# Four-layer fp32 kernel: the convolution's taps all on VectorE, GELU in one piece, and a new order of the steps

## The reference

```python
z = rms_norm_2(x, norm_g) @ w_in
o_a = fox_attention(q, k, v, ff + fox_b) * silu(f_gate)        # 4 heads, causal, with decay
o_b = conformer_conv(glu_in, ...) * silu(c_gate)
o_c = nsa_attention(...) * silu(n_gate)                        # 8 heads, 2 groups, 3 branches
x = x + concat([o_a, o_b, o_c]) @ w_out

def conformer_conv(u, conv_w, conv_b, ln_g, ln_b, w_pw):
    a, b = split(u, 2); y = a * sigmoid(b)                     # 256 channels
    y = causal depthwise convolution of y with 31 taps + conv_b
    return silu(layer_norm(y, ln_g, ln_b)) @ w_pw

def compress(x, pe, w1, w2):      # for k and for v: 15 windows of 32 tokens, in 2 groups
    blk = x[windows] + pe
    return gelu(blk @ w1) @ w2
```

## Time and profile before

| | us |
|---|---|
| median of 3 runs | 1629.15 |
| lowest, highest | 1629.04, 1633.23 |
| the profiled execution | 1630.12 |
| its span, first to last instruction | 1628.2 |
| TensorE busy | 1585.0 |
| VectorE busy | 1066.8 |
| ScalarE busy | 825.1 |
| GpSimd busy | 258.8 |

### The profile page before, as it was taken

How to read it: one execution, slowest core, us unless ns; L and a number is a source line. 1 busy time by engine, 2 the same in 40 slices (tenths; PEclk the granted TensorE clock), 3 DMA queues, 4 the chain that set the end, 5 groups by cost and what they waited for, 6 DMA issues and landing times.

```text
span 1628.2 us, 27282 instructions
## 1 busy us (share of the span) xinstructions
PE 1585.0 (97%) x11240; PEld 1435.0 (88%) x11240; DVE 1066.8 (66%) x1269; ACT 825.1 (51%) x1123; POOL 258.8 (16%) x208
## 2 busy tenths in 40 slices
PE   7999999999999999999999999999999999999997
PEld 7999888888989999999988888898999898879885
DVE  4655557765865555655565867576555589968995
ACT  5443446653454343544454665345444465656563
POOL 0000060010000000000035001000000059405930
PEclk9999999999999999999999999999999999999999
DMA  7757555342555656556746534354656466147512
GB/s 227 231 183 234 177 182 171 124 139 81 179 181 185 203 182 204 168 197 194 237 156 183 163 109 143 106 193 150 218 187 197 124 220 193 33 137 223 192 33 91
DMA packets 206613, 273.97 MB, mean 168 GB/s; under 512 B 18775, under 2 KB 167097, under 8 KB 206009
## 3 DMA queue, kind: packets, MB, share of 16 engines
q1 hardware_dynamic: 206376, 272.67, 52.3%
q10 hardware_dynamic: 144, 0.00, 0.0%
HBM read 271.61 MB, written 1.08 MB: 167 GB/s over the span
## 4 chain that ended last, share of the span: by engine, by line
PE 83%; DVE 11%; ACT 3%; issue 2%; POOL 1%; DMA 0%; SPq 0%; POOLq 0%; ACTq 0%; DVEq 0%
PE bank L506 28%; PE bank L555 14%; PE bank L991 8%; PE bank L980 7%; PE bank L2043 4%; PE bank L1181 3%; DVE wlo L438 3%; PE bank L2299 2%; PE bank L1263 2%; PE bank L2021 2%; PE bank L1124 1%; ACT whi L427 1%; PE bank L1099 1%; DVE hT_lo L357 1%; PE bank L2196 1%
## 5 line engine op out<-in xcount | busy, mean ns | idle before, releaser
L438 DVE TENSOR_TENSOR wlo<-raw,whi 128x2048 fp32r<-128x2048 f32 (+2 forms) x258 | 585.1, 2271 | 327.1 <-ACT whi L427 326.2
L427 ACT ACTIVATE whi<-raw 128x2048 fp32r<-128x2048 f32 (+2 forms) x258 | 484.7, 1881 | 294.2 <-PE bank L555 101.1
L506 PE MATMUL bank<-hT_hi,whi 128*128 128x256 f32 x1408 | 391.6, 278 | 1.3 <-DVE wlo L438 1.0
L506 PE MATMUL bank<-hT_lo,whi 128*128 128x256 f32 x1408 | 389.8, 277 | 0.0
L506 PE MATMUL bank<-hT_hi,wlo 128*128 128x256 f32 x1408 | 389.7, 277 | 0.0
L506 PEld LDWEIGHTS bank<-hT_hi,whi 128*128 128x128 f32 x1408 | 264.7, 188 | 3.0 <-DVE wlo L438 1.8
L506 PEld LDWEIGHTS bank<-hT_lo,whi 128*128 128x128 f32 x1408 | 265.3, 188 | 0.0
L506 PEld LDWEIGHTS bank<-hT_hi,wlo 128*128 128x128 f32 x1408 | 264.7, 188 | 0.0
L555 PE MATMUL bank<-whi,Y 128*128 128x512 f32 (+1 forms) x748 | 224.1, 377 | 0.0
L555 PEld LDWEIGHTS bank<-whi,Y 128*128 128x128 f32 x748 | 140.2, 188 | 28.0
L311 POOL TENSOR_TENSOR st<-st 128x1 f32<-128x1 f32 x18 | 18.0, 1009 | 919.4 <-ACT X L304 919.4
(11 more groups left out here) (398 smaller groups left out, 2824.9 us busy)
## 6 DMA issues: line engine op xcount, KB each, us to landing
raw<-in_ffn_w SPq DMA_DIRECT2D x132, 1024.0 KB, 5.5
raw<-in_w_in SPq DMA_DIRECT2D x80, 1024.0 KB, 5.5
raw<-in_w_out SPq DMA_DIRECT2D x16, 1024.0 KB, 4.9
...
```

The costliest lines, as they stand in the source:

```text
L427: act.activation(m["whi"][:, slot, 0:w], m["raw"][:, slot, 0:w], ACT.Copy).then_inc(s.hi_ready, 1)
L438: dve.tensor_tensor(m["wlo"][:, slot, 0:w], m["raw"][:, slot, 0:w], m["whi"][:, slot, 0:w].bitcast(F32), ALU.subtract).then_inc(s.lo_ready, 1)
L506: mm = pe.matmul(B[bank][:, mt * T:(mt + 1) * T], a, b, start=(n == 0 and k == 0), stop=(n == KK - 1 and k == 2))
```

## The change

Six things change in both second-kind layers.

1. The convolution's half 0 leaves GpSimd. VectorE does all 62 taps. Even and odd taps of each half go to accumulators of their own, four chains in all, and a tap waits only for the tap of its chain; two adds join them. A step `taps.k` now has four operations.
2. GELU for keys and values is one set of operations on 32 x 512 in place of two on 32 x 256.
3. K of the compression is copied, rotated and transposed (`cmp_kt`, a step of its own on TensorE, before `value.0`) ahead of V's copies; the zeros are written much earlier (`cmp_zero`). The ten products of constants go.
4. The scaling and the epsilon of the variance move from GpSimd into VectorE's copy in `ln.1`.
5. VectorE's order: the three maxima of an item stand ahead of taps, `prob.0` comes before `lo.11`, `cmp_score` ahead of `tall.5`, `lo.19` ahead of `ln.1`.
6. ScalarE's order: `exp.0-2` directly behind `hi.10`, both `tok_b` copies and then `gelu` ahead of the turns, `tall.5` behind `turn.2`, and `cmp_prob` behind `exp.5`.

```diff
@@ -110,9 +110,15 @@
         self.eng, self.sem, self.n = eng, sem, 0
 
     def __call__(self, ins):
+        self.until(self.step(ins))
+
+    def step(self, ins):
         self.n += 1
         ins.then_inc(self.sem, 1)
-        self.eng.wait_ge(self.sem, self.n)
+        return self.n
+
+    def until(self, n):
+        self.eng.wait_ge(self.sem, n)
 
 
...
@@ -255,13 +261,13 @@
...
     y_ready=3, ln_var=1, ln_scaled=1, ln_silu=1, ln_split=2, pw_gated=1, pw_split=1, params_in=144,
-    bias_zero=1, conv_step=60, ln_rs=1)
+    bias_zero=1, ln_rs=1)
...
@@ -1855,23 +1861,23 @@
 
 PE2 = words("""
     xt.0 fv.0-1 params fv.2 xt.1 fv.3-15 sm tall.3-4 tall.0 tall.1-2 sg w1.0 scores.0 w1.1 tok.1 tok_b.1 w1.2 tok.0 w1.3
-    tok_b.0 turn.0 tall.5 turn.1 hid_turn turn.2 cmp_kv value.0 heads_turn cmp_score scores.1 tall.6 scores.2 cmp_turn
+    tok_b.0 turn.0 tall.5 turn.1 hid_turn turn.2 cmp_kv heads_turn cmp_kt value.0 cmp_score scores.1 tall.6 scores.2 cmp_turn
     tall.7 turn.3 scores.3 turn.4-5 tall.8 turn.6-7 scores.4 ln.0 turn.8 value.1 ln.1 turn.9 value.2 ln.2 turn.10-11 wo.0-2
     turn.12 wo.3 pw turn.13 wo.8-9 turn.14 wo.10 value.3-4 wo.11 wo.4-6 wo.12-13 wo.7 wo.14-15
 """)
 ACT2 = words("""
-    hh.0-1 sq.1 hh.2-15 hi.2 params hi.3 sm hi.4 decay hi.5 fox_own tall.4 hi.6 tall.0 hi.7 blk.0-1 hi.8 tall.1-2 hi.9-12 exp.0 fv
-    hi.13-14 exp.1 hi.15-16 exp.2 tok_b.1 gelu.0 tok_b.0 turn.0 gelu.1 turn.1 tall.5 hid_turn turn.2 hi.17 heads_turn hi.18
-    cmp_prob exp.3-5 tall.6 cmp_turn exp.6-8 hi.19 tall.7 turn.3 exp.9 turn.4 exp.10 turn.5 exp.11 out.0 hi.20 turn.6 hi.21
+    hh.0-1 sq.1 hh.2-15 hi.2 params hi.3 sm hi.4 decay hi.5 fox_own tall.4 hi.6 tall.0 hi.7 blk.0-1 hi.8 tall.1-2 hi.9-10 exp.0-2
+    hi.11-12 fv hi.13-16 tok_b.1 tok_b.0 gelu turn.0-1 hid_turn turn.2 tall.5 heads_turn hi.17 hi.18
+    exp.3-5 cmp_prob tall.6 cmp_turn exp.6-8 hi.19 tall.7 turn.3 exp.9 turn.4 exp.10 turn.5 exp.11 out.0 hi.20 turn.6 hi.21
     tall.8 turn.7 ln_square exp.12 turn.8 exp.13 turn.9 exp.14 ln_tanh turn.10-11 out.1 ln_high hi.22 turn.12-14 hi.23
     conv_out hi.24 out.2
 """)
 DVE2 = words("""
     hl.0-2 scale.1 hl.3-14 lo.1 hl.15 lo.2-3 sm lo.4 decay fox_bias lo.5 tall.4 lo.6 tall.0 blk.0-1 blk_low.0 lo.7 blk_low.1 lo.8
-    taps.0 lo.9 taps.1 peak.0 taps.2-3 lo.10-12 taps.4-5 sg lo.13 peak.1 taps.6 lo.14 peak.2 taps.7 lo.15 gelu.0 prob.0 gelu_out.0
-    gelu.1 lo.16 gelu_out.1 rotate cmp_kv tall.5 cmp_score lo.17 cmp_shift peak.3 taps.8-9 peak.4-5 cmp_prob tall.6 prob.1
-    peak.6-8 taps.10-11 lo.18 prob.2 taps.12 peak.9 taps.13 peak.10 taps.14 peak.11 taps.15 out.0 prob.3 tall.7 peak.12
-    out_low.0 ln.0 peak.13 tall.8 peak.14 ln.1 lo.19 ln.2 out.1 prob.4 ln_silu lo.20 ln_split lo.21 out_low.1 lo.22 conv_out
+    cmp_zero taps.0 lo.9 peak.0-2 taps.1-2 lo.10 prob.0 lo.11-12 taps.3-4 sg lo.13 taps.5 lo.14 taps.6 lo.15 gelu lo.16 gelu_out
+    rotate cmp_kv cmp_score tall.5 taps.7 peak.3-5 cmp_shift lo.17 cmp_prob tall.6 prob.1
+    peak.6-8 taps.8-9 lo.18 prob.2 taps.10 peak.9 taps.11-12 peak.10 taps.13 peak.11 taps.14-15 out.0 prob.3 tall.7 peak.12
+    out_low.0 ln.0 peak.13 tall.8 peak.14 lo.19 ln.1 ln.2 out.1 prob.4 ln_silu lo.20 ln_split lo.21 out_low.1 lo.22 conv_out
     conv_low out.2 lo.23 out_low.2 lo.24
 """)
 UNITS2 = {"tok": 1, "tok_b": 1, "tall": 1, "sm": 1, "w1": 1, "pw": 1}
@@ -1932,6 +1938,7 @@
     cd = G[:, 3136:3648].rearrange("p (i t) -> p i t", i=2)
     cu = G[:, 3648:4160].rearrange("p (i t) -> p i t", i=2)
     cw = G[:, 4160:4672].rearrange("p (i t) -> p i t", i=2)
+    cacc_odd = cw[:, 0, :], G[:, 5696:5952]
     PcT = G[0:64, 4672:5696].rearrange("p (i q) -> p i q", i=4)
...
@@ -2217,17 +2224,13 @@
                                        start=(kk == 0), stop=(kk == 1))
             mm.then_inc(s.cmp_done, 1)
 
-        def idle_products(n):
-
-            for _ in range(n):
-                pe.matmul(B[0][:, 0:P], ident, ident, start=True, stop=True)
-
-        def cmp_score():
-
-            idle_products(6)
+        def cmp_kt():
+
             pe.wait_ge(s.kcmp_ready, past.kcmp_ready + 1)
             pe.transpose(B[6][:, 128:192], kc2, ident[0:64, 0:64]).then_inc(s.kcmpT_done, 1)
-            idle_products(4)
+
+        def cmp_score():
+
             pe.wait_ge(s.vcmp_ready, past.vcmp_ready + 2)
             pe.wait_ge(s.heads_ready, past.heads_ready + 1)
...
@@ -2432,9 +2435,9 @@
             tile = (0, 4, 6)[k]
             act.activation(Y[:, tile:tile + 2, 0, :], yf.rearrange("p (i q) -> p i q", i=2), ACT.Copy).then_inc(s.yhi_ready, 1)
 
-        def gelu(v):
-            act.wait_ge(s.gelu_in, past.gelu_in + v + 1)
-            act.activation(gl_t[:, v, :], gl_t[:, v, :], ACT.Tanh, scale=float(np.sqrt(2 / np.pi))).then_inc(s.gelu_tanh, 1)
+        def gelu():
+            act.wait_ge(s.gelu_in, past.gelu_in + 1)
+            act.activation(gl_t, gl_t, ACT.Tanh, scale=float(np.sqrt(2 / np.pi))).then_inc(s.gelu_tanh, 1)
 
         def hid_turn():
...
@@ -2584,19 +2587,28 @@
                     ins = TTo(lo, blk[:, v, 8 * q:8 * q + 8, g, 0:N_CMP], hi.bitcast(F32), ALU.subtract)
             ins.then_inc(s.blk_split, 1)
 
+        tap_done = [[0, 0], [0, 0]]
+
         def taps(k):
 
-            acc = cacc[:, 1, :]
             for j in range(2 * k, min(2 * (k + 1), TAPS)):
-                src, w = padded[:, 1, j:j + T], conv_p[:, 1, j:j + 1]
                 if j == 0:
                     dve.wait_ge(s.gate_ready, past.gate_ready + 1)
                     dve.wait_ge(s.par_ready, past.par_ready + 1)
-                    chain(dve.tensor_scalar(acc, src, w, conv_p[:, 1, TAPS:TAPS + 1], ALU.mult, ALU.add))
-                elif j < TAPS - 1:
-                    chain(STT(acc, src, w, acc, ALU.mult, ALU.add))
-                else:
-                    STT(acc, src, w, acc, ALU.mult, ALU.add).then_inc(s.conv_ready, 1)
+                for c in range(2):
+                    acc, src, w = (cacc[:, c, :], cacc_odd[c])[j % 2], padded[:, c, j:j + T], conv_p[:, c, j:j + 1]
+                    if j == 0:
+                        ins = dve.tensor_scalar(acc, src, w, conv_p[:, c, TAPS:TAPS + 1], ALU.mult, ALU.add)
+                    elif j == 1:
+                        ins = dve.tensor_scalar(acc, src, w, None, ALU.mult)
+                    else:
+                        chain.until(tap_done[c][j % 2])
+                        ins = STT(acc, src, w, acc, ALU.mult, ALU.add)
+                    tap_done[c][j % 2] = chain.step(ins)
+            if j == TAPS - 1:
+                for c in range(2):
+                    chain.until(max(tap_done[c]))
+                    TTo(cacc[:, c, :], cacc[:, c, :], cacc_odd[c], ALU.add).then_inc(s.conv_ready, 1)
 
         def peak(j):
...
-            TTo(t_, t_, f, ALU.mult).then_inc(s.gelu_in, 1)
-
-        def gelu_out(v):
-            f, t_ = gl_f[:, v, :], gl_t[:, v, :]
-            dve.wait_ge(s.gelu_tanh, past.gelu_tanh + v + 1)
-            STT(f, t_, 1.0, f, ALU.add, ALU.mult).then_inc(s.gelu_ready, 1)
-
-        def cmp_kv():
+            chain(dve.tensor_copy(gl_f, h))
+            chain(TTo(gl_t, gl_f, gl_f, ALU.mult))
+            chain(dve.tensor_scalar(gl_t, gl_t, 0.044715, 1.0, ALU.mult, ALU.add))
+            TTo(gl_t, gl_t, gl_f, ALU.mult).then_inc(s.gelu_in, 1)
+
+        def gelu_out():
+            dve.wait_ge(s.gelu_tanh, past.gelu_tanh + 1)
+            STT(gl_f, gl_t, 1.0, gl_f, ALU.add, ALU.mult).then_inc(s.gelu_ready, 1)
+
+        def cmp_zero():
             chain(dve.memset(kc2, 0.0))
             chain(dve.memset(kcT, 0.0))
+
+        def cmp_kv():
             dve.wait_ge(s.cmp_done, past.cmp_done + 1)
+            rows = [slice(32 * g, 32 * g + N_CMP) for g in range(2)]
             for g in range(2):
-                rows = slice(32 * g, 32 * g + N_CMP)
-                dve.tensor_copy(kc2[rows, 0:64], B[7][rows, 0:64])
-                for odd in range(2):
-                    ins = dve.tensor_copy(vc[32 * odd:32 * odd + N_CMP, g], B[7][rows, 64:128])
-            ins.then_inc(s.vcmp_ready, 1)
-            dve.wait_ge(s.vcmp_ready, past.vcmp_ready + 1)
+                ins = dve.tensor_copy(kc2[rows[g], 0:64], B[7][rows[g], 0:64])
+            chain(ins)
             chain(rotate(kc2[:, 0:64].rearrange("p (t h n) -> p t h n", t=1, h=1), 1,
                          C("cos_cmp")[0:64, :], C("sin_cmp")[0:64, :]))
             dve.tensor_copy(kc2[:, 64:128], kc2[:, 0:64]).then_inc(s.kcmp_ready, 1)
+            for g in range(2):
+                for odd in range(2):
+                    ins = dve.tensor_copy(vc[32 * odd:32 * odd + N_CMP, g], B[7][rows[g], 64:128])
+            ins.then_inc(s.vcmp_ready, 1)
 
         def cmp_score():
...
@@ -2709,7 +2722,7 @@
                 ins.then_inc(s.ln_centred, 1)
             elif i == 1:
                 dve.wait_ge(s.ln_done, past.ln_done + 2)
-                dve.tensor_copy(st[:, 40:42], B[6][:, 0:2]).then_inc(s.ln_var, 1)
```

(27 more changed lines are left out.)

17 lines of the change are left out of this document (6 added, 11 removed).

## The result

| | us |
|---|---|
| before, median of 15 runs | 1629.33 (1628.16 to 1633.23) |
| after, median of 15 runs | 1635.88 (1631.62 to 1643.35) |
| ratio | 1.0047, 95% interval 1.0036 to 1.0057 |
| profiled execution of after | 1642.15, span 1640.4 |

The change makes the kernel slower by 0.4 to 0.5%. The forecast was 1634.5 with a range of 1626 to 1641. The runs fall into two groups: ten lie between 1631.6 and 1637.0 at mean granted clocks of 0.992 to 0.996, five between 1641.3 and 1643.4 at 0.988 to 0.990. The profiled execution is one of the five.

What follows compares the result with a forecast made beforehand. It took VectorE's list from `peak.3` to `ln.0` as the bound in the second-kind layers: +3.6 us for two layers and +1.7 for the clock, 5.3 on 1630.12, 1635.4, less 0.97 for the median: 1634.5, range 1626 to 1641.

Steps and rivals of the forecast that it cites:

- The pace of a tap: VectorE's taps in independent chains start every 0.39 us, ends 0.335 and 0.52; all 62 take 24.2 us.
- The rival by which a split would not help: Each of the 30 taps behind `peak.3` costs 0.13 us more, 3.9 us a layer, 1642 us; chance 0.07.
- the rule that the prediction gave for it: Trainium skill: VectorE's next operation starts only when the pipeline is empty, so a tap would stay at 0.52 us.
- The lead of TensorE: `turn.0` directly follows `tok_b.0`, `scores.1` some 13 us behind it: TensorE 3.7 us ahead. Rival that it lasts: 1617, chance 0.13.
- The K branch: K's copies and rotation done 1.4 us behind `cmp_kv`; rival that they stay slow: up to 1.9 us per layer, 1638, chance 0.08.
- The two idle spells of VectorE: VectorE waits for TensorE 2.9 us at `cmp_kv` and 2.4 us at `peak.3`, and never from there until `ln.0`.
- The list: VectorE's work from `peak.3` to `tall.7` sums to 35.3 us, putting `ln.0` 3.4 us late; this forecast's chance 0.55.
- TensorE's waits for it: TensorE waits for VectorE about 3 us ahead of `ln.0` and 3 more in `cmp_turn`, `turn.7` and `scores.4`.
- From `ln.0` to `ln.2`: TensorE's own work takes 6.94 us, where before it took 8.31 with a 1.37 us wait for GpSimd.
- The clock: Low clock after TensorE's wait ahead of `ln.0` costs up to 1.7 us a layer; half taken, 0.85 each, +1.7 in all.
- If the granted clock shows a long low stretch: Sign in the new profile that the prediction is wrong; the low stretch was taken as 4 us.
- Contention with GpSimd: GpSimd's operations slow VectorE's between 1390.6 and 1418.6, worth some 1.5 us there; VectorE work ahead of 1371 is hidden.

Runs made afterwards that it cites:

- experiment 2: The changed kernel with one accumulator per half, two chains in place of four and no joining adds: 1634.12 us against 1630.47 before, ratio 1.0020.
- experiment 1: The changed kernel with half 0 of the convolution back on GpSimd and half 1 as one chain on VectorE: 1628.48 us against 1630.47 before, ratio 0.9994.
- 6: The changed kernel with 29 of half 0's 31 taps left out, output not the reference's: 1622.08 us against 1630.04 before, ratio 0.9948.
- experiment 3: The changed kernel with 16 more taps ahead of `peak.3`, where VectorE idles (the filled order): 1620.64 us against 1630.47 before, ratio 0.9949.
- experiment 7: The kernel before with only the variance scaling and epsilon moved into VectorE's copy, behind `lo.19`: 1627.69 us against 1630.04 before, ratio 0.9985.
- experiment 10: The changed kernel with repeated or constant TensorE products sized to fit its waits: 1634.17 us against 1629.91 before, ratio 1.0027.
- experiment 9: The changed kernel with added TensorE products, 20 of them ahead of the wait at `ln.0`, which outlasted it: 1642.02 us against 1629.18 before, ratio 1.0079.
- experiments 11: The changed kernel with half 0 back on GpSimd and half 1's taps in the places of experiment 3: 1634.86 us against 1629.18 before, ratio 1.0041.
- 12: The same as experiments 11 with 30 of GpSimd's 31 taps left out, half 0 not computed: 1620.41 us against 1629.91 before, ratio 0.9940.

## Why the prediction was right

**The pace of a tap.** Forecast 0.39, measured 0.396. Right: the value came from the start of the next instruction behind the last tap, and the independent pair of rows 5, 0.335 with the scalar's 0.055 added, agrees. The rival by which a split would not help, and with it the rule that the prediction gave for it, is refuted for these taps. But the four chains are not needed for it: two do as well (experiment 2).

**The lead of TensorE.** `turn.0` directly behind `tok_b.0`, and `scores.1` 13 us later: measured no gap and 13.4. The K branch is as fast as forecast. The two idle spells of VectorE, 2.9 and 2.4 forecast, are 2.70 and 2.23. One reading was too smooth: ahead of 1371 TensorE does wait in the kernel before, 0.33, 0.24 and 0.61 us at the start of the layer, in the stretch of rows 7. VectorE's taps come later than that, so the forecast does not change.

**The list.** Forecast 35.3 us from `peak.3` to `tall.7`, measured 35.3. `ln.0` was to come 51.0 us behind `tok_b.0` (1371.04 to 1422.0), and comes at 51.3. TensorE's waits for it were to be 6 us a layer and add up to 6.1, but they are shared out otherwise: ahead of `ln.0` 0.78 and 2.83 us, not 3 in each, because in the first layer the low clock stretches `scores.4` into that wait. That this list makes the kernel slower, and not another part of the change, is shown by undoing it in three ways: half 0 on GpSimd (experiment 1), left out (6), or the same taps in other places (3). VectorE's subtractions all last 2.27 to 2.29 us in the changed kernel's attention items, as the forecast had it.

**From `ln.0` to `ln.2`.** Forecast 6.94, measured 6.88 with the clock at 1.00 (experiments 7 and 10). The wait for GpSimd is gone. `ln.2` was to be at 58.0 us and is at 58.2 in experiment 10, which makes 2.3 and 1.7 us for the two layers against 2.1 and 1.5: 4.0 in all against 3.6. The median of experiment 10 is 4.3 above that of before.

**The clock.** This is the term that was off in size, the 1.7 us for both layers, and the weakest step: half of an upper bound. In the median it measures 2.3 us (6.55 above before in the changed kernel, 4.26 in experiment 10) and by the two ratios 3.3. Their intervals overlap, and an estimate from them leaves anything from 0.6 to 6 us. In the profiled execution it is far more: `ln.0` to `ln.2` takes 10.56 and 13.04 us instead of 6.89, 3.7 and 6.2 more, about half of the 7.8 and 13.0 us of low clock that lie there. I had bounded it by 4 us of low clock a layer; the stretch lasted 13.6. "If the granted clock shows a long low stretch" was one of the signs of being wrong, and for this execution it came true; the five runs above 1641 lie outside the range. So the list was forecast by its mechanism, but that the clock's half bound came near to its share in the median is luck.

The sum for the profiled execution closes. The span is 12.2 longer. Of this the list is 1.9 and 1.8 (experiment 10 against before: from one `tok_b.0` to the next 165.2 and 163.3, from the second to the end 95.6 and 93.9), the clock 3.6 and 6.2 (168.8 and 165.2; 101.8 and 95.6), less 1.3 by which it came to the end of the first `tok_b.0` earlier: 1.9 + 1.8 + 3.6 + 6.2 - 1.3 = 12.2. That last is no gain of the change. The layer began 0.5 us later than before, and the low stretch of 3.4 us in the kernel before from 1298.2 on the earlier trace rows, worth 1.7 us at half the clock, is not in this execution. It is in some executions of either kind: the profile of experiment 7 has it, and so has that of experiment 9, which is built on the changed kernel.

The median landed 1.4 us above the forecast. Of this 0.2 is the kernel before, whose median is 1629.33 in 15 runs and was 1629.15 in 3, 0.4 the list, and the 0.8 left goes to the clock by subtraction.

**Contention with GpSimd.** I valued it at 1.5 us between 1390 and 1418 and as hidden ahead of 1371. For this change that was enough. But it made me price GpSimd's rest too low in general: it is worth 14 us in the filled order, where VectorE has only 0.9 us of idle time left between 1325 and 1371 (experiments 11 and 12). With GpSimd at rest VectorE's free time lay ahead of `peak.3` (3.4 us between 1325 and 1371, then 2.70 and 2.23), and the change put 30 of 62 taps behind it. That is why it lost what experiment 3 gains.
